# Sixteen input-projection slabs as seven block products each, with weight sums made by accumulating transfers

## The reference

```
h = rms_norm(x, norm_mix[l])
proj = h @ w_in[l]
u_s5, x_lru, g_lru, p_rw, z_ssd, xbc_ssd, dt_ssd = _split(
    proj, [S5_W, LRU_W, LRU_W, RW_COLS, SSD_W, SSD_XBC, SSD_HEADS])
```

```
mag = jnp.exp(lr * dt)
abar_re, abar_im = mag * jnp.cos(li * dt), mag * jnp.sin(li * dt)
_, _, st_re, st_im = lax.associative_scan(
    _complex_affine_combine, (a_re, a_im, bu_re, bu_im), axis=1)
```

## Time and profile before

| | |
|---|---|
| median of three runs | 2472.53 us |
| profiled execution | 2467.88 us, of which the span is 2465.9 us |
| PE busy | 2275.0 us, 92% of the span |
| DVE, ACT, POOL busy | 870.9, 376.5, 513.8 us |
| end of the last fast product | 596.7 us |
| multiplies of the 20 plain tiles | 640 records, 279.1 us |
| multiplies of the 8 fast slabs | 896 records, 196.4 us |

### The profile page before, as it was taken

One profiled execution on the slowest core, in us unless ns is written; L12 is line 12 of the kernel. 1 busy time (PEld: TensorE's weight loads), 2 busy tenths in 40 slices (PEclk: granted clock), 3 DMA queues, 4 the chain that ended last, 5 costly groups with the idle time before them and its releaser, 6 DMA issues.

```text
span 2465.9 us, 32922 instructions
## 1 busy us (share of the span) xinstructions
PE 2275.0 (92%) x12955; PEld 1226.1 (50%) x12955; DVE 870.9 (35%) x1319; ACT 376.5 (15%) x658; POOL 513.8 (21%) x636
## 2 busy tenths in 40 slices
PE   8999999999999999899988888888888988888888
PEld 4444448886566646544444444444444444444443
DVE  5799876557544332411111111111111111111114
ACT  3000152215222222000000000000000000000002
POOL 3566316541322110111111101101111111110110
PEclk9999999999999999999999999999999999999999
DMA  6222213323202345999999999999999999999998
GB/s 190 69 68 68 74 52 94 86 70 101 97 26 79 112 162 202 368 421 427 425 425 426 426 425 426 427 425 426 427 426 426 427 426 424 427 426 425 425 426 361
DMA packets 151301, 717.78 MB, mean 291 GB/s; under 512 B 34264, under 2 KB 89884, under 8 KB 107452
## 3 DMA queue, kind: packets, MB, share of 16 engines
q1 hardware_dynamic: 123416, 693.51, 69.0%
q0 software_dynamic: 18432, 16.83, 2.0%
q10 hardware_dynamic: 9380, 6.40, 0.8%
HBM read 719.68 MB, written 47.19 MB: 311 GB/s over the span
## 4 chain that ended last, share of the span: by engine, by line
PE 48%; DMA 42%; DVE 7%; issue 1%; POOL 0%; ACT 0%; DVEq 0%; POOLq 0%; ACTq 0%
DMA big<-in_moe_w 42%; PE ps L2956 11%; PE ps L2618 8%; PE ps L2678 6%; PE ps L2583 6%; DVE big L1514 3%; PE ps L2987 3%; PE ps L2833 2%; PE ps L2753 1%; PE ps L2972 1%; PE ps L2738 1%; DVE big L1646 1%; DVE big L1645 1%; PE ps L2997 1%; PE ps L2632 1%
## 5 line engine op out<-in xcount | busy, mean ns | idle before, releaser
L2956 PE MATMUL ps<-big 128*64 128x384 f32 x4096 | 696.3, 495 | 105.4 <-DMA big<-in_moe_w 94.1
L2956 PEld LDWEIGHTS ps<-big 128*64 128x64 f32 x4096 | 308.9, 138 | 499.6 <-issue 318.4
L2987 PE MATMUL ps<-big 128*64 128x512 f32 x1536 | 376.9, 643 | 56.9 <-DVE big L2313 56.9
L2583 PE MATMUL ps<-big 128*128 128x512 f32 (+1 forms) x672 | 293.2, 594 | 0.0
L2309 DVE TENSOR_SCALAR big<-ps,scal 128x384 f32<-128x384 f32 x64 | 39.6, 619 | 702.4 <-PE ps L2956 698.3
L2987 PEld LDWEIGHTS ps<-big 128*64 128x64 f32 x1536 | 122.7, 147 | 264.0 <-issue 233.0
L2318 DVE SCALAR_TENSOR_TENSOR big<-ps,scal,big 128x512 f32<-128x512 f32 x128 | 90.2, 747 | 389.3 <-PE ps L2987 389.3
L2583 PEld LDWEIGHTS ps<-big 128*128 128x128 f32 (+1 forms) x672 | 125.6, 189 | 163.8 <-issue 163.7
L1039 POOL COPY scal<-slots 128x3 f32 (+1 forms) x64 | 11.8, 186 | 900.7 <-DVE big L2318 886.0
L2618 PE MATMUL ps<-big 128*128 128x256 f32 x896 | 196.4, 379 | 0.0
L2618 PEld LDWEIGHTS ps<-big 128*128 128x128 f32 x896 | 169.5, 190 | 24.8 <-issue 2.3
(11 more groups left out here) (435 smaller groups left out, 1982.1 us busy)
## 6 DMA issues: line engine op xcount, KB each, us to landing
big<-in_moe_w SPq DMA_DIRECT2D x187, 3072.0 KB, 39.0
big<-in_w_in SPq DMA_DIRECT2D x10, 2048.0 KB, 8.3
big<-in_w_in SPq DMA_DIRECT2D x32, 512.0 KB, 3.8
big<-in_moe_w SPq DMA_DIRECT2D x6, 1536.0 KB, 23.5
big<-in_w_out SPq DMA_DIRECT2D x8, 1024.0 KB, 5.4
big<-y_rows SPq DMA_DIRECT2D x8, 1024.0 KB, 27.5
big<-in_x SPq DMA_DIRECT2D x4, 1024.0 KB, 8.6
big<-in_x SPq DMA_DIRECT2D x16, 256.0 KB, 3.6
```

Source lines behind the costliest of these rows:

```text
L2583: last = nc.tensor.matmul(ps[n % 2][0:wd, :], ring[s % 2][:, k, c:c + wd], hT[:, k, :], start=(k == 0), stop=(k == NC - 1))
L2956: last = nc.tensor.matmul(ps[2 + w][B * g:B * g + B, 0:FF], xT[k][:, j, B * g:B * g + B], W13[k][w][:, NJ * g + j, :], start=(j == 0), sto ...
L2987: last = nc.tensor.matmul(ps[5 + q][B * g:B * g + B, :], hid[k][:, m, :], W2[k][:, m, 512 * n:512 * n + 512], start=(m == 0), stop=(m == F ...
```

## The change

- **Sixteen of the eighteen wide slabs go the fast way** (eight before). The plain slabs are now the two of S5 and the low-rank slab, which comes third. The sixteen fast slabs come in the order XL (2), GL (2), XBC (4), Z (2), R (2), K (2), V (2).
- **Weight sums by transfers.** SP loads all seven operands of a slab into eight rotating slots of 512 KB (slot of product g is g modulo 8). POOL issues four accumulating transfers: `sum1` adds A22 from memory to the loaded A21, `sum2` adds S1 (on-chip) to A11, `sum3` adds A11 from memory to A21, `sum4` adds S2 (on-chip) to A12. Signs move into the activations' sums and into ACT's `scale=-1.0`. No weight sum is left on a compute engine.
- **Activation sums T1, T2, T4** move from behind the LRU convolution to the front of POOL's list, ahead of the S5 tables and of the copies into `Gin`.
- **S5 tables.** POOL now adds the two angles (in turns) and takes off whole turns, three operations (`wrap`). ACT makes the cosine and the sine from that (`table`, three activations).
- **Places.** `s5_inputs` and `s5_outputs` sit within the third tile, an S5 step comes every 24 units (a 256-token product is one, a 512-token product two), and the LRU, S5 and SSD pieces sit at new places among the products. `Z_END` is 10, and from there on the pieces stand as far from the end as before.

```
-        slabs = [(C_S5 + SW * i, SW) for i in range(C_R // SW)] + [(C_XBC + SW * i, SW) for i in range((C_DT - C_XBC) // SW)] \
-            + [(C_LORA, LW + LA + LG)]
-        fast_slabs = [C_Z + SW * i for i in range(W // SW)] + [C_R + SW * i for i in range(3 * W // SW)]
+        slabs = [(C_S5 + SW * i, SW) for i in range(W // SW)] + [(C_LORA, LW + LA + LG)]
+        fast_slabs = [C_S5 + W + SW * i for i in range((C_R - C_S5 - W) // SW)] + [C_XBC + SW * i for i in range((C_DT - C_XBC) // SW)] \
+            + [C_Z + SW * i for i in range(W // SW)] + [C_R + SW * i for i in range(3 * W // SW)]
...
+            for f in range(NF):
+                for b in range(PB_):
+                    g = PB_ * f + b
+                    if g == 0:
+                        sp.wait_ge(proj_ok, NT - 2)
+                    elif g == 4:
+                        sp.wait_ge(proj_ok, NT)
+                    elif f:
+                        sp.wait_ge(prod_ok, PROD + g - PB_ + 1)
+                    sp.dma_start(slot(f, b), weights(f, parts[b])).then_inc(weight_in[b], 16)
...
+            nc.gpsimd.tensor_tensor(T1, B11, B12, sub)
+            nc.gpsimd.tensor_tensor(T2, B12, B22, sub).then_inc(side_ok, 1)
...
+            def wrap(p):
+                cosT, sinT = (s5tab[:, 2 * (p % 2) + r, :] for r in range(2))
+                if p >= 2:
+                    pool.wait_ge(tab_used, p - 1)
+                g.do(nc.gpsimd.tensor_tensor(cosT.rearrange("p (a b) -> p a b", a=COARSE), ...
+                g.do(nc.gpsimd.tensor_scalar(sinT, cosT, MAGIC, MAGIC, ALU.add, sub))
+                nc.gpsimd.tensor_tensor(sinT, cosT, sinT, sub).then_inc(wrap_ok, 1)
...
             def sum1(f):
-                pool.wait_ge(a_in["A21"], A_IN["A21"] + 16 * (f + 1))
-                pool.wait_ge(a_in["A22"], A_IN["A22"] + 16 * (f + 1))
-                weight_sum(f, "S1", "A21", "A22", ALU.add)
+                weight_in_wait(f, B_S1)
+                nc.gpsimd.dma_start(slot(f, B_S1), weights(f, "A22"), accum_op=ALU.add).then_inc(s1_in, 16)
+
+            def sum2(f):
+                weight_in_wait(f, B_S2)
+                pool.wait_ge(s1_in, 16 * (f + 1))
+                nc.gpsimd.dma_start(slot(f, B_S2), slot(f, B_S1), accum_op=ALU.add).then_inc(s2_in, 16)
...
+                    if b == 0 and f:
+                        sum4(f)
+                    if b == 3 and f < NF - 1:
+                        sum1(f + 1)
...
+                    p, off = divmod(PB_ * f + b + 12, 3)
+                    if off == 0 and p < NPAIR:
+                        wrap(p)
...
+            def table(p):
+                cosT, sinT = (s5tab[:, 2 * (p % 2) + r, :] for r in range(2))
+                act.wait_ge(wrap_ok, WRAP + p + 1)
+                a.do(nc.scalar.activation(cosT, sinT, ACT.Abs))
+                a.settle()
+                nc.scalar.activation(sinT, sinT, ACT.Sin, scale=6.283185)
+                nc.scalar.activation(cosT, cosT, ACT.Sin, scale=-6.283185, bias=halfpi[:]).then_inc(tab_ok, 1)
...
                 for k in range(8):
-                    last = nc.tensor.matmul(o, w[:, k, :], side[:, k, :], start=(k == 0 and b in (0, 1, 3)), stop=(k == 7),
+                    last = nc.tensor.matmul(o, w[:, k, :], side[:, k, :], start=(k == 0 and b in (0, 1, 5)), stop=(k == 7),
                                             skip_group_check=True)
+                    s5_at(76 + 8 * g + k)
```

More of the change, by code:

```diff
@@ L502, in build, with slabs_done @@
         T3 = B12
-        products = [("A11", B11), ("A12", B21), ("S2", T2), ("S1", T1), ("S3", T3), ("S4", B22), ("A22", T4)]
+        sides = [B11, T1, T2, B22, T3, B21, T4]
+        parts = ["A11", "A21", "A11", "A12", "A21", "A12", "A22"]
+        B_S1, B_S2, B_S4, B_S3 = 1, 2, 3, 4
         def bank_of(f, b):
             return ps[(f + b) % 2][:, 0:TH]
-        fast_out = [Z_[:, q, :] for q in range(WT)] + [R_[:, q, :] for q in range(WT)] + [K_[:, q, :] for q in range(WT)] \
-            + [V_[:, q, :] for q in range(WT)]
+        fast_out = [x[:, q, :] for x in (XL, GL, XBC[:, 0:4], XBC[:, 4:8], Z_, R_, K_, V_) for q in range(WT)]
+        XL_END, GL_END, X_END, Z_END, R_END, K_END = 2, 4, 4, 10, 12, 14
+        def slabs_done(eng, n):
+            eng.wait_ge(took, TOOK + PB_ * n)
+            eng.wait_ge(added, ADDED + 3 * n)
         def block_out(f, n, t):
@@ L911, in sum4 @@
+            def sum2(f):
+                weight_in_wait(f, B_S2)
+                pool.wait_ge(s1_in, 16 * (f + 1))
+                nc.gpsimd.dma_start(slot(f, B_S2), slot(f, B_S1), accum_op=ALU.add).then_inc(s2_in, 16)
+            def sum3(f):
+                weight_in_wait(f, B_S3)
+                nc.gpsimd.dma_start(slot(f, B_S3), weights(f, "A11"), accum_op=ALU.add).then_inc(s3_in, 16)
             def sum4(f):
-                pool.wait_ge(a_in["A12"], A_IN["A12"] + 16 * (f + 1))
-                pool.wait_ge(sum_ok, SUMS + 4 * f + 3)
@@ L914, in sum4 @@
-                weight_sum(f, "S4", "A12", "S2", sub)
+                weight_in_wait(f, B_S4)
+                pool.wait_ge(s2_in, 16 * (f + 1))
+                nc.gpsimd.dma_start(slot(f, B_S4), slot(f, B_S2), accum_op=ALU.add).then_inc(s4_in, 16)
             def add_held(f, k):
-                n, t, reads = ((0, 0, 2), (1, 1, 5), (0, 1, 6))[k]
+                n, t, reads = ((0, 1, 4), (1, 1, 5), (0, 0, 6))[k]
                 pool.wait_ge(took, TOOK + PB_ * f + reads)
                 o = block_out(f, n, t)
-                nc.gpsimd.tensor_tensor(o, o, held[(0, 2, 1)[k]], ALU.add).then_inc(added, 1)
+                nc.gpsimd.tensor_tensor(o, o, held[(1, 2, 0)[k]], ALU.add).then_inc(added, 1)
@@ new lines, in _ @@
+                for b in range(PB_):
+                    if b == 0 and f:
+                        sum4(f)
+                    if b == 3 and f < NF - 1:
+                        sum1(f + 1)
+                    if b == 4:
+                        add_held(f, 0)
+                    if b == 5:
+                        add_held(f, 1)
+                        if f == Z_END:
+                            pool.wait_ge(dtv_ok, 2)
+                            k, i = at[("xt", NTT - 1)]
+                            pool.wait_ge(full[k], i + 1)
+                            triangle(0)
+                            triangle(1)
+                        if f < NF - 1:
+                            sum2(f + 1)
+                    if b == 6:
+                        add_held(f, 2)
+                        if f < NF - 1:
+                            sum3(f + 1)
+                        if f in (Z_END + 1, Z_END + 2):
+                            triangle(f - Z_END + 1)
+                    p, off = divmod(PB_ * f + b + 12, 3)
+                    if off == 0 and p < NPAIR:
+                        wrap(p)
@@ L1131, in take_product @@
                     if f:
[L1133 removed]
+                        act.wait_ge(added, ADDED + 3 * f - (0, 2, 1)[b // 2])
                     to = held[b // 2]
                 else:
[L1136 to L1139 removed]
+                    if b == 1 and f in (R_END, K_END):
+                        act.wait_ge(away_out, AWAY_OUT + 16 * (1 if f == R_END else 2))
+                    to = block_out(f, *{1: (1, 1), 3: (0, 1), 5: (0, 0), 6: (1, 0)}[b])
+                nc.scalar.activation(to, bank_of(f, b), ACT.Copy, scale=-1.0 if b in (1, 4, 6) else 1.0).then_inc(took, 1)
             act.wait_ge(setup_ok, S5COL)
```

326 lines of the change are left out of this document (139 added, 187 removed).

## The result

| | time, us | against before, 95% interval |
|---|---|---|
| before | 2471.51 median of 18 runs | |
| after | 2475.35 median of 18 runs | 1.0022 [1.0015, 1.0029] |
| predicted | 2455.0 (2446 to 2484) | 0.993 |

The change costs 4 to 5 us where 17.5 were to be gained: the kernel did not get faster. The time is inside the range, and the difference is inside the 0.3% that the prediction counted as no change. But the likeliest case (62%, up to 2463) did not come, for two reasons that I had priced too low.

The account below looks back on a forecast made before the run. PE was taken to bound the stage, with DVE close to full in the S5 part. -26.9 + 5.7 + 1.5 + 2 = -17.7 us, rounded to -17.5, gave 2455.0 us, range 2446 to 2484.

Parts of the forecast that it names:

- the likeliest case: Whole kernel: the main forecast with its own range, 2446 to 2463 us, given 62%.
- The products: PE's list: eight slabs change from plain (27.91 us) to fast (24.55 us), 26.9 us less.
- The front wait: Third tile: PE idles until Gin is ready behind POOL's sums and wraps, 5.7 us, between 3.7 and 9.
- First products: First fast products: the table for pair 4 comes late from POOL, delaying ACT and PE; 1.5 us, between 0 and 5.
- DVE's pairs: S5 part: DVE's pairs at 12.1 us tie with PE's 12.0; 2 us charged, between 0 and 5.
- The weight sums: Fast slabs: issue, landing and engine load of the four accumulating transfers a slab stay hidden, cost 0.
- if accumulating costs nothing extra: Transfer-engine load: on this condition seven loads and four sums need 21.9 us in a slab of 24.55.
- m: Cost of an accumulating transfer as a multiple of a plain one; a slab needs 13.9 + 8.0 m us.
- The third rival: Every fast slab: accumulating transfers fill the transfer engines; 2478 us at m = 2, 2514 at m = 2.3; 13%.
- The prediction's own sign of being wrong: Slabs after the S5 part: PE waits for weight sums, with the transfer engines' share near 1.0.
- the second rival: POOL's issue time goes by rows, 8.4 us, delaying S5 slabs, sum4 and the start; some +18 us, 2473 us; 12%.

Follow-up runs that it names:

- e11: The e8 kernel without any weight sums, so products read the plain blocks; median 2446.88 us, ratio 0.9910 against before.
- e8: The changed kernel with T1 and T2 left in place and the other three activation-sum operations put behind the Gin copies; median 2463.21 us, ratio 0.9977 against before.
- e1: The changed kernel with all five activation-sum operations put behind the copies into Gin; ratio 0.9996 against before.
- e12: The e8 kernel with the block of sum1 loaded one product earlier and sum1 issued at product 2 (was 3); median 2457.59 us, ratio 0.9947 against before.
- e14: The e12 kernel with each slab's sum3 also issued behind its sum4 instead of ahead of it; ratio 0.9938 against before.
- e9: The e8 kernel with the second and fourth weight sum of slabs 6 to 15 as GpSimd additions instead of accumulating transfers; ratio 0.9975 against before.

## Why the prediction was wrong

- *The products, -26.9 us: right.* 64 records take 13.98 us, 0.218 us each. In e11, in which nearly nothing else is left, PE is busy 26.4 us less than before from 15 us to the last product (581.19 and 554.79). That product ends 24.5 us earlier, with 2.5 us of idle time ahead of it. The time fell by 22.2 us.
- *The front wait, +5.7: wrong, 13.14, and the step that failed is the one that put contention on POOL.* I wrote that POOL beside DVE takes up to 2.06 us for 1.05 us and added 2 us to POOL's list. The end of the sums (52.3) and PE's demand (59.7, measured 59.56) were right. The row of 2.06 us is of L874, which takes 1.27 us in the first two pairs of tables and not 1.05. I never asked what the sums do to DVE, although the S5 angles are DVE's and POOL's wraps wait for them. They came at 59.0, 6.8 us after the sums' end. The two wraps took 9.1 us instead of 6.8, mostly since each holds a TENSOR_SCALAR of 1.95 us that I had at 1.05; that this fits the 2 us added for contention is luck. Both together are the 9.2 us by which Gin was later than 63.4. e8 shows it by its removal: there the small operations take 0.17 us, the first wrap starts at 46.66 instead of 59.17, and PE waits 0.48.
- *First products, +1.5: 0 in after, 0.9 us in e8 and 3.0 in e1,* where no front wait covers it. The term was real and hidden by the larger one.
- *DVE's pairs, +2: inside its 0 to 5.* PE never waits for an S5 pair in after; its 0.40 us for DVE are for the convolution. The pairs come 12.6 us apart from 90 to 228 us, 12.1 forecast. A gain that moves the front makes them visible (1.1 us of waits in e11): DVE is busy 48 of 50 us in the S5 part of every variant.
- *The weight sums, 0: wrong, some 15 us, and the dearer of the two steps that failed.* The issue was priced well enough (4 us for the two from memory; 3.2 measured), the landing was not: 6 us taken, 8 to 9 measured. Behind this stands the term "if accumulating costs nothing extra". That was the lower end of an unknown, and I let the forecast rest on it although the count left only 2.6 us of a 24.55 us slab free, so that anything over m = 1.3 had to break slabs 7 to 9. A bound between 1 and 3 with nothing in the trace to choose by deserved more than 13%. The third rival was the right mechanism. Its own arithmetic, at the m that was measured, gives 12 us for the 10.1 of waits, but the total agrees in part by luck: it puts 1.2 us on the S5 slabs and 11.1 on slabs 7 to 9, and the trace has 6.6 and 3.5.
- *The clock.* The waits cost more than their length: the 6.8 us by which PE's busy time in after exceeds that of e11, which has the same multiplies, at a granted clock of 0.98 against 1.00 from 15 us to the last product. The prediction had no term for it. The rows show it behind the 13.14, 3.04 and 2.92 us waits (1.97 for 1.04 us, and clocks of 0.86 to 0.97 in their stretches). It is not a matter of length alone: in e8 the ten multiplies behind 4.12 us were slow (3.41 us) and those behind 3.44 us at 268 us were not, 12.76 us for 58.

The last product of after is 28.0 us later than that of e11: 21.2 us of more idle time and these 6.8.

With the front as it came, a wait of 13.1 for 5.7, and the weight sums at some 15 us for 0, the sum becomes -26.9 + 13.1 + 0.4 + 15.3 = +1.9 us, and the slower multiplies behind the front wait come on top (0.9 us at the turning of Gin alone). Measured are +5.4 us by the ratio and 3.5 at the last product. The prediction's own sign of being wrong came true, a share of the transfer engines near 1.0 (1.06 from 350 to 400 us). One slip did no harm: the parts of the second rival add up to 19.7 us, not 18. What stays open: what the chain's head start is worth (e12 and e14), and when a wait is followed by a slow stretch.

## What to carry to other kernels

When work is put on GpSimd, ask first which VectorE operations run beside it and who waits for those. Here a long GpSimd operation cost VectorE up to its whole length however small the VectorE operation was, so put it where VectorE waits anyway. When an addition moves from an engine into a transfer, count the time of the transfer engines and not bytes, and where they are near full, issue first what is wanted first. Where the spare of a resource is less than the span of an unknown price, the case in which it is overrun is not a side case.

## What the runs showed of the hardware

- An accumulating transfer of 512 KB took 3.6 us of all sixteen transfer engines, a plain one on the same queue 1.65 us, in a quarter as many packets, and a plain load through SP 1.94 us. It also held POOL longer at its issue: 1.58 against 0.92 us from memory, 0.90 against 0.57 on the chip.
- VectorE operations stood still for nearly all of a 4.5 us GpSimd operation issued just before, down to 16 columns (4.36 to 4.49 for 0.16 to 0.17 us). The Trainium skill, "SBUF — State Buffer", section "Who interferes with whom", says that the later one of the two fully blocks until the first is done, and that also tensor_scalar can take part; the trace agrees, with 4.37 us for a TENSOR_SCALAR of one input. I had used an average of two stretches in place of this rule: 0.36 us of VectorE per us of GpSimd.
- It works the other way less sharply: GpSimd's addition of 128x1024 took 2.35 us in e9 while VectorE idled (275 us) and 3.27 beside its scans (324 us).
- GpSimd's TENSOR_SCALAR on 512 columns took 1.92 to 1.98 us in the first four wraps of after and of e8 alike, its TENSOR_TENSOR 1.04 to 1.56.
